# Value products of the attention stage, made for two neighbouring units at once

## What is computed

```python
# latent tokens: query block n (128 tokens) against blocks n-1, n, n+1 and the cached context
s_band = einsum('bnqkgd,bnskd->bnkgqs', qb, kb) * scale      # |distance| <= 128 only
s_ctx  = einsum('bnqkgd,bskd->bnkgqs', qb, k_ctx) * scale
p = softmax_with_sink(concatenate([s_band, s_ctx], -1), sink)
out = einsum('bnkgqs,bnskd->bnqkgd', p[..., :nb], vb) + einsum('bnkgqs,bskd->bnqkgd', p[..., nb:], v_ctx)
# context tokens: one query block against its own 128 keys, same softmax
```

## Time and profile before

| | |
|---|---|
| median of 3 runs | 2141.63 us (2139.04 to 2145.55) |
| profiled execution | 2139.24 us, span in the trace 2137.5 us |
| busy share of the span | PE 96%, PEld 84%, DVE 44%, POOL 35%, ACT 30% |
| mean granted clock of PE | 0.973 |
| attention stage in the trace | about 1448 to 1587 us |
| value products (line 710) in the trace | 240 records of 256 columns, as many weight loads |

### The profile page before, as it was taken

The page is one execution under the profiler, slowest core; times in us unless marked ns, Lnnn a source line. Parts: engine busy times, 40 slices in busy tenths (PEclk is TensorE's granted clock), DMA queues, the critical chain, the costliest instruction groups (busy, mean ns, idle before and its releaser), DMA issues.

```text
span 2137.5 us, 32383 instructions
## 1 busy us (share of the span) xinstructions
PE 2042.4 (96%) x12472; PEld 1801.4 (84%) x12472; DVE 930.3 (44%) x1299; ACT 651.8 (30%) x1280; POOL 756.9 (35%) x477
## 2 busy tenths in 40 slices
PE   5899999999999998999999999998979999999998
PEld 2776888598678848999999999895559999999998
DVE  1601420340142034753465264565732773574473
ACT  2422222222321234332232132425533432232232
POOL 2433233233323324333333333536844333333332
PEclk8899999999999998999999999898979999999998
DMA  6432232133223211342333233120002122222211
GB/s 253 167 137 76 99 109 69 60 109 109 79 90 114 74 40 40 138 147 79 109 137 118 102 116 109 67 80 26 1 9 71 60 79 70 78 69 79 79 59 50
DMA packets 52264, 190.02 MB, mean 89 GB/s; under 512 B 5824, under 2 KB 6976, under 8 KB 51520
## 3 DMA queue, kind: packets, MB, share of 16 engines
q1 hardware_dynamic: 47232, 171.99, 23.2%
q10 hardware_dynamic: 4928, 16.53, 2.0%
HBM read 181.41 MB, written 7.08 MB: 88 GB/s over the span
## 4 chain that ended last, share of the span: by engine, by line
PE 89%; issue 2%; ACT 2%; DVE 2%; POOL 2%; DMA 1%; POOLq 1%; DVEq 0%; ACTq 0%; SPq 0%
PE ps L350 35%; PE ps L389 22%; PE ps L365 16%; PE ps L405 2%; PE ps L332 2%; PE ps L541 2%; PE ps L550 1%; PE ps L423 1%; PE ps L536 1%; PE ps L337 1%; ACT pr L1007 1%; PE ps L413 1%; POOL pr L1127 1%; PE ps L691 1%; POOLq L1078 1%
## 5 line engine op out<-in xcount | busy, mean ns | idle before, releaser
L1052 POOL TENSOR_TENSOR w_l<-raw,w_h 128x1024 fp32r<-128x1024 f32 x232 | 563.4, 2430 | 1167.0 <-ACT w_h L746 1166.7
L350 PE MATMUL ps<-h_h,w_h 128*128 128x320 f32 x1696 | 527.6, 311 | 3.6 <-issue 2.1
L350 PE MATMUL ps<-h_h,w_l 128*128 128x320 f32 x1696 | 524.1, 309 | 0.0
L350 PE MATMUL ps<-h_l,w_h 128*128 128x320 f32 x1696 | 524.0, 309 | 0.0
L746 ACT CAST w_h<-raw 128x1024 fp32r<-128x1024 f32 x232 | 245.5, 1058 | 580.1 <-PE ps L389 314.2
L350 PEld LDWEIGHTS ps<-h_h,w_h 128*128 128x128 f32 x1696 | 318.4, 188 | 16.9 <-issue 15.2
L350 PEld LDWEIGHTS ps<-h_l,w_h 128*128 128x128 f32 x1696 | 318.5, 188 | 0.2 <-issue 0.2
L350 PEld LDWEIGHTS ps<-h_h,w_l 128*128 128x128 f32 x1696 | 318.4, 188 | 0.0
L1204 DVE SCALAR_TENSOR_TENSOR xT<-ps,mods,xT 128x128 f32<-128x128 f32 (+2 forms) x264 | 107.9, 436 | 301.3 <-PE ps L389 301.3
L1345 DVE SCALAR_TENSOR_TENSOR cc<-ca,vec,cc 128x641 f32<-128x641 f32 x88 | 230.9, 2624 | 15.2 <-issue 15.2
L389 PE MATMUL ps<-m_h,w_l 128*128 128x320 f32 x704 | 217.0, 308 | 0.0
(11 more groups left out here) (183 smaller groups left out, 2701.4 us busy)
## 6 DMA issues: line engine op xcount, KB each, us to landing
raw<-stream_dram SPq DMA_DIRECT2D x328, 512.0 KB, 3.6
S<-state_dram ACTq DMA_DIRECT2D x4, 1024.0 KB, 7.4
new_state_dram<-st_out ACTq DMA_DIRECT2D x8, 512.0 KB, 3.2
xT<-x_dram ACTq DMA_DIRECT2D x1, 2560.0 KB, 11.7
y_dram<-aq ACTq DMA_DIRECT2D x8, 320.0 KB, 2.4
dm<-diff_dram ACTq DMA_DIRECT2D x1, 512.0 KB, 3.8
rope_t<-rope_t_dram ACTq DMA_DIRECT2D x1, 512.0 KB, 7.2
rope_a<-rope_a_dram ACTq DMA_DIRECT2D x1, 512.0 KB, 3.4
```

The costliest lines, as they stand in the source:

```text
L350: mm = nc.tensor.matmul(ps[:, banks + half, 0:HALF], w, x[:, k, lo_hi(half)], start=(k == 0 and n == 0), stop=(k == KT - 1 and n == 2))
L1052: nc.gpsimd.tensor_tensor(w_l[:, r, :], raw[:, s, :], w_h[:, r, :].bitcast(F32), ALU.subtract).then_inc(raw_used[s], 1)
```

## The change

PE's value products of an even unit are no longer made in that unit's turn. In the odd unit's turn one call makes the product of both units for a key block and a key/value head: its moving operand is `pT[:, :, kb, ...]`, 256 columns of each of the two buffers, and it writes all 512 columns of the bank. The fourth key block's transposes come before all value products. `apv_done` now counts pairs in place of units, and the waits on it are rewritten: the cast of a pair and the copies into `pT` wait for the count of pairs, and the exponentials, which need only `pr`'s buffer back, wait for the transposes (`apt_done`) in place of the values.

```diff
--- before.py
+++ after.py
@@ -698,17 +698,19 @@
                 pe.wait_ge(ap_done, u + 1)
                 for kb in range(min(3, len(kbs))):
                     unit_turn(u, kb)
-                if u % 2 == 0 and u >= 2:
+                if len(kbs) > 3:
+                    unit_turn(u, 3)
+                if u % 2 == 0:
+                    return
+                if u >= 2:
                     pe.wait_ge(aolo_done, u // 2)
                 for kb, src in enumerate(kbs):
-                    if kb == 1 and len(kbs) > 3:
-                        unit_turn(u, 3)
                     wait_pt(pe, PT_AT[u] + kb)
                     val = cv if src is None else av[:, src, :]
                     for r in range(2):
                         kv = 2 * (u // 2 % 2) + r
-                        mm = nc.tensor.matmul(ps[64 * r:64 * r + 64, 7, 256 * (u % 2):256 * (u % 2) + 256],
-                                              val[:, kv * HD:(kv + 1) * HD], pT[:, u % 2, kb, 256 * r:256 * r + 256],
+                        mm = nc.tensor.matmul(ps[64 * r:64 * r + 64, 7, :], val[:, kv * HD:(kv + 1) * HD],
+                                              pT[:, :, kb, 256 * r:256 * r + 256],
                                               start=(kb == 0), stop=(kb == len(kbs) - 1))
                 mm.then_inc(apv_done, 1)
 
@@ -1002,7 +1004,7 @@
                 w, st = P * len(key_blocks(u // KVH)), stat[:, u % 3]
                 act.wait_ge(am_done, 2 * u + half + 1)
                 if u >= 3 and half == 0:
-                    act.wait_ge(apv_done, u - 2)
+                    act.wait_ge(apt_done, PT_AT[u - 2])
                 for g in (2 * half, 2 * half + 1):
                     op = nc.scalar.activation(pr[:, u % 3, g, 0:w], ps[:, g, 0:w], ACT.Exp, scale=HD ** -0.5,
                                               bias=st[:, 1, g:g + 1], accum_out=st[:, 3, g:g + 1])
@@ -1017,12 +1019,12 @@
                 x = PT_AT[u] + kb
                 act.wait_ge(apt_done, x + 1)
                 if u >= 2:
-                    act.wait_ge(apv_done, u - 1)
+                    act.wait_ge(apv_done, u // 2)
                 nc.scalar.copy(pT[:, u % 2, kb, :], ps[:, 4 + x % 3, :]).then_inc(apt_act, 1)
 
             for u in range(UNITS + 3):
                 if u >= 3 and u % 2 == 0:
-                    act.wait_ge(apv_done, u - 2)
+                    act.wait_ge(apv_done, u // 2 - 1)
                     o = (u - 3) // 2
                     nc.scalar.copy(h_h[:, (o % 2) * G:(o % 2) * G + G, tok_of(o // 2)],
                                    ps[:, 7, :].rearrange("p (g q) -> p g q", g=G)).then_inc(aohi_done, 1)
@@ -1415,7 +1417,7 @@
                 x = PT_AT[u] + kb
                 dve.wait_ge(apt_done, x + 1)
                 if u >= 2:
-                    dve.wait_ge(apv_done, u - 1)
+                    dve.wait_ge(apv_done, u // 2)
                 V.tensor_copy(pT[:, u % 2, kb, :], ps[:, 4 + x % 3, :]).then_inc(apt_dve, 1)
 
             def pair_rest(o):
```

## The result

The changed kernel takes 2147.86 us (median of 10 runs, 2145.51 to 2154.41) against 2141.16 (10 runs): a ratio of 1.0035, interval 1.0024 to 1.0046. It is slower, by 5 to 10 us, which is small beside the whole time but clear of the noise. A second measurement of the same two kernels gave 1.0036 (1.0022 to 1.0050). The profiled execution took 2147.86 us with a span of 2146.1.

What follows compares the result with a forecast made beforehand. PE, busy 96% of the span, bounds the kernel; in the attention stage a ring of waits does. Terms of +5.67 us on the profiled 2139.24 gave 2144.9, plus 2.39 for a median 2147.3; range 2140 to 2153.

Steps and rivals of the forecast that it cites:

- three signs of being wrong: A merged block clearly under 0.86 us, transposes of odd units waiting for nothing, or a granted clock below 1 before 1560.
- What a merged call costs: On PE, a merged value block takes 0.86 us; four take 3.60 us to the next scores, three 2.74.
- the cheap-columns rival: Rival: value calls of 512 columns cost little more than 256, a merged block 0.43 us; 2136 in all, chance 0.11.
- What moves: Attention stage: all value products of a pair stand at the odd turn's end; new semaphore counts bring no wait.
- The ring through POOL: Once per pair: DVE's reduction, reciprocal, POOL's odd-unit scaling, transposes, all values, scores, next reduction; 15.39 us for units 6 to 8.
- The rival that POOL is not last: Attention stage: reciprocal comes earlier or odd-turn scores decide, pairs stay even, only 1.30 us remains; about 2143, chance 0.17.
- The first pair: Pair 0 and 1, at the attention stage's start: 1475.22 against 1475.10, so +0.12 us.
- Units 4 to 6: Distance of first reductions: 12.80 us against 13.21 before, counted as 0 because unit 5's scores and copies bound it.
- Units 12 to 14: Distance of first reductions: 14.95 us against 13.74, +1.21, as POOL was already last there.
- 16 to 18: Distance of these units' first reductions: 13.35 us against 12.13, +1.22 (from +0.2 to +2.8), with transposes at the lower clock.
- The end: From 1570.73 to the output projection's first matmul: two pairs of one block at the lower clock, +1.30 us.
- the clock as a rival: PE's granted clock falls one pair earlier and rises later at the attention stage's start: +3.5 us, 2150.8; chance 0.22.

Runs made afterwards that it cites:

- the order alone: Changed kernel with merging undone: all values of a pair at the odd turn's end, each unit in calls of 256 columns; 2150.19 us, ratio 1.0046.
- the halved scaling: POOL scales only two of a unit's four query heads: changed kernel so edited 2140.14 us (0.9992), kernel before so edited 2136.36 us (0.9977).
- the filled kernel: Changed kernel plus unread products on PE, 512 columns ending even turns, 256 ahead of odd turns' transposes; 2146.80 us, ratio 1.0024.

## Why the prediction was right, and where it was not

The forecast was 2147.3 us with a range of 2140 to 2153; the median is 2147.86. Its direction and the ring that it named were right; that the number lies 0.6 us beside the forecast is in part luck, as shown below. Slower had 0.40, same 0.53; the measured ratio is 1.0035 with its interval on both sides of 1.0030, the bound that I set, while the median lies 0.14 us under my bound in us, 2148.0. Which of the two classes came true can't be told. Of my three signs of being wrong one appeared, a granted clock below 1 before 1560 (0.95 from 1476 to 1511), and a second in part: the transposes of units 5 and 15 waited for nothing (they start at 1481.54 and 1557.38, right behind the scores).

*What a merged call costs* was right: four blocks took 3.59 us to the next scores (3.60 forecast), and the cheap-columns rival fell with 592 ns against 379: 213 ns more for 256 columns. The Trainium skill (TensorE: Matmul & The Clock Gate, section Back-to-back issue gap) gives a stream at 512 columns 1.6 times the time of one at 128; here doubling the columns doubled a block's time, 0.43 to 0.86 us or more, so for these float32 calls the measurement decides against that figure. *What moves* was right, shown by two runs: the order alone makes the loss, the fourth block's transposes nothing. *The ring through POOL* was right in mechanism and size where the clock stays up: 15.46, 15.48 and 15.32 against 15.39, 15.39 and 15.23, 15.03 against 14.95 for units 12 to 14 in three of four traces, and with the gaps filled 12.46 against 12.36 for 14 to 16. POOL's wait for the reciprocal became 3.12 us a pair (3.0 forecast). The rival that POOL is not last fell with the halved scaling, for units 6 to 12; for the two distances of 4 to 6 and 14 to 16 it holds.

The terms that were mis-sized are those with a clock in them. The first pair (units 2 to 4) had +0.12 and measured +2.5 to +2.8 in three of four traces, nothing in the first. Units 4 to 6 had 0 and measured +1.8 to +1.9: of these, the filled kernel still has 0.8 at the higher clock, but 0.49 of it is the added product; some 0.3 (an estimate, 0.81 less 0.49) is left for the order itself. Units 12 to 14 had +1.21 and measured +1.3, once +2.8; 14 to 16 had -0.10 and measured +0.8 to +1.05; 16 to 18 had +1.22, within +0.2 to +2.8, and measured +2.3 to +2.6: I took 2.02 us for twelve transposes at the lower clock, from a row in which the clock changed on the way; wholly at the lower clock they took 2.78 at the stage's start (1462.65 in the trace before), and 2.82 here (1570.14). The end, with +1.30, measured +0.8 to +1.1. The stage's sum is therefore +11 to +12 in the traces, twice the +5.67 of the forecast. I had the clock as a rival of its own, at +3.5 more and a chance of 0.22; it came in addition and in every trace. The mistake was to make one outcome or the other of two things that came together. That the timed median nevertheless stands 0.6 us beside the forecast is luck: the sum was some 6 us too small for the stage, and the 4 us that stay open made up for most of it. The right number is no proof of the sum.

## What to carry to other kernels

Making calls wider saved nothing here, where their time goes by columns and their weight loads are hidden; what such a change really did is move work, so price the order, not the calls. Write down each ring of waits with its length, including those that only an engine's own queue closes (here copies ahead of exponentials on ACT), and put movable work where its inputs are old and no queue waits behind it: one block moved by half a turn (with the pair's rest) gained 7 us, all blocks moved by a turn lost 31. Work concentrated in one turn leaves gaps of 1 to 2 us in the other, and here the granted clock fell behind such gaps and did not where they were filled. Look at each distance in more than one trace before giving it a cause: a clock that rose or fell elsewhere moved single distances by 1.5 to 2.8 us between executions of one kernel.

## What was not expected of the hardware

With 1.28 us of products that nobody reads added to each pair of turns, the granted clock was 1.00 in two stretches of 25 us where it had been 0.93 and 0.86, and two distances came down by 1 us each, though PE had more to do. The stage was 6.7 us shorter in that trace, of which a part is chance, and the timed median only 1.1 us lower. A gap of 1.81 us in place of unit 0's value products (1465.4 to 1467.4 before) went with a late rise of the clock in five of six traces and in none of four without it; it came with some 2.5 us each time.
